# The plan of a hand-woven mixer stage: the pace of its last 40 projection products set from 1.85 to 2.17

## The reference, cut to what matters

```python
proj = h @ w_in                      # 1024 x 1024 by 1024 x (3*512 + 4*512 + 16)
q_a, k_a, v_a, q_d, k_d, v_d, z_d, b_d, a_d = split(proj)
y_attn  = dilated_attention(q_a, k_a, v_a, rel_bias)
y_delta = gated_deltanet(q_d, k_d, v_d, z_d, b_d, a_d, ...)
y = concatenate([y_attn, y_delta]) @ w_out
```

## Time and profile before

| | us |
|---|---|
| runs | 3851.53, 3855.84, 3858.59 (median 3855.84) |
| the profiled execution | 3853.3, with a span of 3851.4 |
| PE busy in the span | 3668.9 (95%) |
| the mixer's tiles 2 to 7, from local(2) to the last tile's wT | 2323.15 to 2740.20 |

### The profile page before, as it was taken

One profiled execution on the slowest core, in us unless ns is written; L12 is line 12 of the kernel. 1 busy time (PEld: TensorE's weight loads), 2 busy tenths in 40 slices (PEclk: granted clock), 3 DMA queues, 4 the chain that ended last, 5 costly groups with the idle time before them and its releaser, 6 DMA issues. The chain is left out here.

```text
span 3851.4 us, 45448 instructions
## 1 busy us (share of the span) xinstructions
PE 3668.9 (95%) x17861; PEld 1944.9 (50%) x17861; DVE 1726.1 (45%) x2962; ACT 932.3 (24%) x1937; POOL 470.8 (12%) x364
## 2 busy tenths in 40 slices
PE   7999998999999899999979999999898999999999
PEld 4554444555544444444435558765654444444444
DVE  3579998655555200000012335455452433333246
ACT  2311111554232212222124213222342311111001
POOL 0032234211000011121110111111000000000000
PEclk8979999999999799999989999999799999999999
DMA  4213232121554699999965222222103111111334
GB/s 175 77 50 123 77 120 74 63 72 29 194 187 176 232 340 335 331 338 330 340 191 192 101 68 91 76 82 101 37 12 123 47 44 44 44 44 44 123 115 161
DMA packets 291768, 520.24 MB, mean 135 GB/s; under 512 B 23932, under 2 KB 102868, under 8 KB 290302
## 3 DMA queue, kind: packets, MB, share of 16 engines
q1 hardware_dynamic: 272878, 467.74, 35.2%
q0 software_dynamic: 12976, 43.54, 4.0%
q10 hardware_dynamic: 5728, 6.37, 0.5%
HBM read 454.07 MB, written 63.53 MB: 134 GB/s over the span
## 5 line engine op out<-in xcount | busy, mean ns | idle before, releaser
L1762 PE MATMUL jn_duo<-space,dsa 128*128 128x512 f32 x1024 | 452.8, 595 | 4.9 <-ACT dsa L1830 4.9
L608 PE MATMUL ch_side<-aT,space 128*128 128x512 f32 x896 | 391.7, 596 | 0.0
L1859 DVE SCALAR_TENSOR_TENSOR dsa<-jn_duo,ex_weight,ex_gate 128x1024 f32<-128x1024 f32 x32 | 41.1, 1284 | 635.1 <-PE jn_duo L1778 635.1
L1762 PEld LDWEIGHTS jn_duo<-space,dsa 128*128 128x128 f32 x1024 | 193.1, 191 | 236.3 <-issue 236.3
L608 PEld LDWEIGHTS ch_side<-aT,space 128*128 128x128 f32 x896 | 168.5, 190 | 213.4 <-issue 210.7
L3067 PE MATMUL en_bank<-en_h,en_up 128*128 128x512 f32 x528 | 233.8, 592 | 0.0
L1778 PE MATMUL jn_duo<-aT,dsa 128*128 128x512 f32 x512 | 225.1, 592 | 0.7 <-ACT dsa L1841 0.7
L733 DVE MAX8 ch_best<-ch_score 128x8 f32<-128x384 f32 (+5 forms) x192 | 171.6, 894 | 6.1
L2236 PE MATMUL mx_duo<-mx_chunks,mx_region 128*128 128x512 f32 x384 | 170.8, 598 | 0.4 <-ACT mx_outs L2506 0.4
L734 DVE MATCH_REPLACE8 ch_score<-ch_best,ch_score 128x384 f32<-128x384 f32 (+5 forms) x192 | 168.1, 876 | 0.0
L3067 PEld LDWEIGHTS en_bank<-en_h,en_up 128*128 128x128 f32 x528 | 100.2, 190 | 125.8 <-issue 125.8
(11 more groups left out here) (539 smaller groups left out, 5658.9 us busy)
## 6 DMA issues: line engine op xcount, KB each, us to landing
space<-exp_w SPq DMA_DIRECT2D x64, 2048.0 KB, 13.2
aT<-exp_w SPq DMA_DIRECT2D x32, 2048.0 KB, 15.1
en_up<-w_down SPq DMA_DIRECT2D x132, 256.0 KB, 3.5
space<-ada_w SPq DMA_DIRECT2D x12, 2048.0 KB, 11.1
space<-w_ada SPq DMA_DIRECT2D x12, 2048.0 KB, 8.3
mx_x<-proj_padded SPq DMA_DIRECT2D x96, 256.0 KB, 3.6
aT<-w_in SPq DMA_DIRECT2D x7, 2048.0 KB, 8.7
en_up<-w_gate SPq DMA_DIRECT2D x22, 512.0 KB, 4.9
```

The lines of the kernel that those rows point to most:

```text
L608: last = nc.tensor.matmul(side_ps[i % 2][:, 0:width], hT[:, k, t * P:(t + 1) * P], by[:, k, 0:width], start=k == 0, stop=k == KD - 1)
L1762: last = nc.tensor.matmul(ps[:, :], xT[b][:, k, :], w13[b][s][:, k, :], start=k == 0, stop=k == KD - 1)
```

## The change

One constant. `B_STRETCH` is a factor on the distance in the plan between two of the last 40 jobs: for 256 wide ones it goes from 6.475 to 7.595 plan units, for 512 wide ones from 12.95 to 15.19. The first of them keeps its place, 217.5; the last goes from 567.2 to 627.6. No instruction is added or removed.

```diff
--- before.py
+++ after.py
@@ -1900,7 +1900,7 @@
 N3_PACE = 5.6
 A_START, A_PACE = 46.0, 24.5
 B_START = A_START + 7 * A_PACE
-B_STRETCH = 1.85
+B_STRETCH = 2.17
 D_START, D_PACE = 53.0, 70.0
 LINE_AT, LINE_STEP = 26.0, 2.4
 LOCAL_AT, LOCAL_STEP = 36.0, 2.25
```

## The result

The changed kernel is slower: a median of 3874.79 us (3868.85 to 3879.86, 5 runs) against 3851.53 us (3849.97 to 3858.59, 5 runs), a ratio of 1.0058, 95% interval 1.0047 to 1.0070; by the ratio that is about 22 us. I had forecast 3848.8 us, 7 us less than the median of the three runs that I had of the kernel before, and a range up to 3861. The profiled execution took 3868.85 us with a span of 3867.0; it is the fastest of the five, so its differences are a little small.

What follows compares the result with a forecast made beforehand. PE, busy 3668.9 of 3851.4 us, was taken as the bound, losing only to standing still and half clock. Terms -3.5 - 4.3 + 0.8 = -7.0 us gave 3846.3 from the profiled 3853.3, or 3848.8 against the median; range 3838 to 3861.

Steps and rivals of the forecast that it cites:

- The price of each block: On PE, a 512 wide job costs 7.05 us, a 256 wide one 3.55, one tile's narrow steps 29.2.
- the sum of the prediction: Periods 2 to 7 together would go down from 417.1 us to about 410.
- Period 7: Last tile, given four 512 wide jobs: loss beyond jobs and narrow steps falls from 16.1 to 12.6, 3.5 us won.
- Period 4: Jobs between steps 3 and 7 remove the wait for M (4.9): loss 14.0 to 9.7, 4.3 us won.
- I take the sum: Period 6 would last 64.0 us, its jobs, narrow steps and old loss added, though conv might hold it longer.
- 0.8 given back: Extra loss where jobs move to other places: 0.3 us in period 6 and 0.5 in period 5.
- DVE is busy 42 of 71 us there, so there is room: In period 6, argument that DVE has idle time for conv's work, though conv's steps stand in one row with local's.
- My own sign of being wrong: Listed signs included period 6 or 2 at 68 us with longer waits on L2759 or L2808.
- The first: More is won: period 7's loss is 8, not 12.6, and scan(7) gains 3 us; 3841 us, chance 0.17.
- The second: Half clock at period 7's start stays 11.4 us whatever stands there, M's wait hides in it; 3852 us, chance 0.15.
- The third: Conv is the bound: no tile with conv goes below 68.0 us, 7.0 given back; 3855.8 us, chance 0.08.
- The fourth: Slower: in the last tile the clock stays 0.50 until the second job's end, +12 us; 3868 us, chance 0.10.

Runs made afterwards that it cites:

- the run with better places: Three wide jobs moved a few plan units within periods 4 and 6 of the kernel before, nothing beside the last tile: 3843.05 us, ratio 0.9985.
- the kernel with good places: The changed kernel's job counts per period kept, its wide jobs moved to places where they cover waits: 3849.70 us, ratio 0.9999 to the kernel before.
- the first run: From the changed kernel, one wide job in each of periods 4, 5 and 6 moved to the front of step 23: 3872.52 us, ratio 1.0050 to before.

## Why the prediction was wrong

**The price of each block** held: in the run with better places period 5 kept a clock of 1.00 and lasted 66.73 us, and five jobs (35.25), 29.2 and its idle time of 2.41 make 66.9.

**Where the error is.** By the sum of the prediction periods 2 to 7 should have lasted about 410 us; they lasted 435.6. Of the 25.5 us between, 15.8 are in periods 2, 3, 5 and 6, 6.8 in period 4 and 3.0 in period 7.

**Period 7** was nearly right in its waits. M's wait was forecast at 2.56 us and measured at 2.56; three of the four waits at the end stayed, 0.88, 0.78 and 0.79, and that of 1.1 on L2804 went; POOL's grew from 0.95 to 1.82. I set its loss at 12.6, of which 7.1 idle, and it was 15.6 (73.02 - 28.2 - 29.2), of which 7.12 idle. What was too small is the half clock: 5.5 us forecast and 8.5 measured, where it had been 11.4. The clock came back behind the first waits only to fall again, as these windows ahead of the wait for M and behind it show:

```profile
2697.00:2707.00 10.00, 8.69 (x109) 5.27 (x107) 3.33 (x5) 1.63 (x3) 1.77 (x1) 0.99 0.01 2
2707.50:2717.00 9.50, 8.62 (x68) 6.41 (x69) 3.47 (x7) 0.59 (x1) 0.00 (x0) 0.50 0.01 2
```

I had priced a fall of the clock by the earlier trace rows, where a job follows 1.9 us behind the wait. Here 5.0 us of narrow products stand between POOL's wait and the first job, and 5.3 between M's and the second, all at half clock:

```profile
2687.13 1.11 PE L2273 MATMUL mx_duo<-ident,mx_early 128*128 128x128 f32 x4 [1.82 <-POOL mx_early L2646]
...
2692.09 9.29 PE L2240 MATMUL mx_duo<-mx_region,mx_chunks 128*128 128x512 f32 x16
...
2713.59 8.79 PE L2240 MATMUL mx_duo<-mx_region,mx_chunks 128*128 128x512 f32 x16
```

Half of 5.0 and of 5.3, and what the two jobs took above 7.13, are 9.0 us, near the 8.5.

**Period 4** was forecast to win its wait for M back, and it did: no wait on L2791 is left. I had it at a loss of 9.7 us and it was 16.5, as L2808 made PE wait 4.38, where it had made no wait before, and the clock was 0.94.

**Periods 2, 3, 5, 6** hold the step that failed: "I take the sum", with "0.8 given back". It took the cover of conv's work as unchanged as long as jobs were in the period. The losses of the four were 8.4, 5.7, 8.4 and 14.9 us where I had 4.7, 5.9, 4.1 and 6.9; in period 2 the wait on L2808 went from 1.7 to 3.0 and one of 1.6 on L2830 came. I had the mechanism in hand: the prediction says that 2.41 us of wait are conv's work standing in front of L2808. But I carried it along as a property of the period, and counted the jobs in a period, not the places where they stand. In the tiles with conv I listed job places against steps 3 and 7 only. The same list for steps 17, 23 and 25, against conv's places on DVE, would have shown that the fourth job of period 5 moves from 50.5 to 51.9, past step 23 at 51.75, and that the third of period 6 moves from 32.3 to 42.7, past the products that wait for the copy L2804, which DVE does behind conv and y. The argument "DVE is busy 42 of 71 us there, so there is room" also misread its row: 42.26 is the busy time of the weight loads, DVE's is 37.99. So DVE has more idle time than I said, and still it was late where PE needed it. My own sign of being wrong came true: period 6 above 68 with a longer wait on L2808.

**The rivals.** The first, a last tile nearly without loss, is what the kernel with good places shows, but the changed kernel does not have those places. The second, the half clock that stays, was half true: 8.5 of 11.4 us stayed, but M's wait did not hide. Its rule that jobs change nothing is not what the runs show, as period 7 ran at 0.97 with four jobs in good places. The third, conv as a floor of 68 us, named the right strand and the wrong law: periods of 63.6 and 56.3 us with four and three jobs exist when they stand right. The fourth, slower by a half clock over two whole jobs, had the direction and not the cause: the two jobs took 9.29 and 8.79 us and not 14, and most of the loss lay in the periods before. The measured time lies above all four, also above the 3868 of the fourth: none had a wait that grows because a job moved past it.

The change does what it says, and what it is for is not wrong in itself: put right, jobs beside the last tile cost less than their work (16.6 us for 28.2). What it also does, unnamed, is to shift some thirty other jobs against DVE's bursts.

## What to carry to other kernels

In a plan written by hand, filler work has two values: the time it takes, and the wait it stands over. Changing a spacing keeps the first and deals the second anew, so the effect jumps (1.85, 2.0 and 2.17 gave 1, 1.0127 and 1.0058): list each filler against the steps whose operand comes from an engine with other work in front, and pin it there. Look at the waits in the window that such an edit touches, since timed runs with a few us of clock noise hid a wait of 5 us here; but a wait that is gone is not yet time won, as the first run shows, where half clock took it back.

## What the runs showed that I had not expected

TensorE's clock follows more than busy time. In period 7 of the kernel before, PE was busy 14.82 of 15 us and stayed at 0.50; the same tile with one wide job in it and one shortly ahead of it ran at 0.96 and was 3.7 us shorter, with 7.05 us more to do. And with the same order of PE's instructions in it period 7 took 68.6 us at 0.88 in one kernel and 61.9 at 0.97 in another, which had a job at 572.0 just ahead and fewer waits. What exactly brings the clock back was not settled; no run here isolates it, and part of the difference can be that of two executions.
